# An FFN whose up projections use seven products for a 2x2 block, with each down visit in two halves

## What is computed

```python
h = _rms(x, norm_g[l, 2]) * (1.0 + scale_f) + shift_f
a, g = jnp.split(h @ ffn_w_in[l], 2, axis=-1)          # 2048 -> 2 x 5632
x = x + (gate_f * _rms((jax.nn.silu(a) * g) @ ffn_w_out[l], norm_g[l, 3])).astype(x.dtype)
```

## Time and profile before

| | |
|---|---|
| median of 3 runs | 2585.65 us (2585.51 to 2586.03) |
| span of the profiled execution, first to last instruction | 2583.7 us |
| PE, DVE, ACT, Pool busy | 99%, 78%, 53%, 10% of the span |
| instructions | 34752, of them 12080 matmuls |
| data moved | 611 MB, mean 237 GB/s |

### The profile page before, as it was taken

The page is one execution under the profiler, slowest core; times in us unless marked ns, Lnnn a source line. Parts: engine busy times, 40 slices in busy tenths (PEclk is TensorE's granted clock), DMA queues, the critical chain, the costliest instruction groups (busy, mean ns, idle before and its releaser), DMA issues.

```text
span 2583.7 us, 34752 instructions
## 1 busy us (share of the span) xinstructions
PE 2564.6 (99%) x12080; PEld 2129.4 (82%) x12080; DVE 2003.3 (78%) x2580; ACT 1369.5 (53%) x1809; POOL 252.5 (10%) x312
## 2 busy tenths in 40 slices
PE   9999999999999999999999999999999999999998
PEld 8888888888888887888888777888788888888887
DVE  6898788788878889876686888787856666666898
ACT  6545566656665656455556444444644444444444
POOL 0021022223222000080000000000000000000000
PEclk9999999999999999999999999999999999999999
DMA  9667788878787986756555775799566666666785
GB/s 319 227 216 253 228 278 265 282 256 309 255 288 252 318 275 211 265 172 224 174 178 168 254 242 195 247 313 319 175 205 194 192 192 194 193 191 192 259 299 191
DMA packets 278364, 611.08 MB, mean 237 GB/s; under 512 B 19916, under 2 KB 21136, under 8 KB 276336
## 3 DMA queue, kind: packets, MB, share of 16 engines
q1 hardware_dynamic: 273696, 583.53, 69.2%
q0 software_dynamic: 4416, 26.13, 2.8%
q10 hardware_dynamic: 144, 0.01, 0.0%
HBM read 599.08 MB, written 11.29 MB: 236 GB/s over the span
## 4 chain that ended last, share of the span: by engine, by line
PE 92%; DVE 4%; ACT 1%; DMA 1%; issue 1%; SPq 0%; DVEq 0%; ACTq 0%
PE ps L670 92%; DMA w_raw<-in_w_in 1%; DVE w_lo L2111 1%; DVE arena L2106 1%; ACT w_hi L1338 1%; PE ps L807 0%; DVE arena L3104 0%; DMA w_raw<-in_ffn_w_out 0%; PE ps L828 0%; DVE arena L2132 0%; DVE x L2132 0%; ACT arena L1379 0%; PE ps L1254 0%; DVE x L2106 0%; DVE mod_parts L2254 0%
## 5 line engine op out<-in xcount | busy, mean ns | idle before, releaser
L1338 ACT ACTIVATE w_hi<-w_raw 128x1024 fp32r<-128x1024 f32 (+1 forms) x898 | 948.3, 1057 | 1135.5 <-PE ps L670 1037.4
L2111 DVE TENSOR_TENSOR w_lo<-w_raw,w_hi 128x1024 fp32r<-128x1024 f32 x809 | 1001.3, 1240 | 473.0 <-ACT w_hi L1338 468.8
L670 PE MATMUL ps<-w_hi,hop_part 128*128 128x512 f32 x4264 | 1334.2, 391 | 3.2 <-DVE w_lo L2111 2.0
L670 PEld LDWEIGHTS ps<-w_hi,hop_part 128*128 128x128 f32 x4264 | 800.3, 188 | 176.4 <-issue 5.1
L670 PE MATMUL ps<-w_lo,hop_part 128*128 128x512 f32 x2132 | 829.6, 389 | 0.0
L670 PEld LDWEIGHTS ps<-w_lo,hop_part 128*128 128x128 f32 x2132 | 400.3, 188 | 81.5
L670 PE MATMUL ps<-w_hi,hid_hi_part 128*128 128x512 f32 x992 | 387.1, 390 | 0.0
L670 PE MATMUL ps<-w_lo,hid_hi_part 128*128 128x512 f32 x992 | 386.0, 389 | 0.0
L670 PE MATMUL ps<-w_hi,hid_lo_part 128*128 128x512 f32 x992 | 386.0, 389 | 0.0
L2106 DVE SCALAR_TENSOR_TENSOR arena<-arena,cs 128x768 f32<-128x768 f32 x240 | 245.9, 1025 | 0.3
L670 PE MATMUL ps<-hop_part,w_hi 128*128 128x512 f32 (+1 forms) x992 | 236.1, 380 | 2.0 <-ACT w_hi L1338 1.1
(11 more groups left out here) (335 smaller groups left out, 1352.5 us busy)
## 6 DMA issues: line engine op xcount, KB each, us to landing
arena<-in_ada_w SPq DMA_DIRECT2D x256, 384.0 KB, 5.2
w_raw<-in_ffn_w_in SPq DMA_DIRECT2D x176, 512.0 KB, 4.4
w_raw<-in_w_up SPq DMA_DIRECT2D x128, 512.0 KB, 4.3
w_raw<-in_w_down SPq DMA_DIRECT2D x128, 512.0 KB, 4.9
w_raw<-in_w_gate SPq DMA_DIRECT2D x128, 512.0 KB, 4.4
w_raw<-in_ffn_w_out SPq DMA_DIRECT2D x88, 512.0 KB, 4.5
w_raw<-in_w_out SPq DMA_DIRECT2D x64, 512.0 KB, 5.3
w_raw<-in_wide_columns SPq DMA_DIRECT2D x64, 512.0 KB, 4.1
```

What stands on the lines that cost most here:

```text
L670: return nc.tensor.matmul(o, w, r, start=start, stop=stop, skip_group_check=True)
L1338: return nc.scalar.activation(o, i, ACT.Copy, scale=scale)
L2111: V.tensor_tensor(w_lo[:, j % LEAD, :, 0:cols], w_raw[:, j % RAW, :, 0:cols], w_hi[:, j % LEAD, :, 0:cols].bitcast(F32), ALU.subtract).the ...
```

## The change

The up projections of eight of the eleven blocks are computed in another form. Activations (two halves of 128 tokens) and weights (two halves of a unit's rows; gate columns and up columns side by side) are seen as 2x2 blocks, and their product is made from seven block products instead of eight, with sums of blocks on both sides. One gate unit and the up unit of the same rows form a group (64 groups). Its seven pieces of weights are `11`, `12`, `s2`, `s4`, `s1`, `s3`, `22`; each gets three matmuls into a bank of its own, so that seven PSUM banks are held through a block and the eighth, `VISIT_BANK`, takes the down projection and the transposes.

Pool makes the sums: four sums of activation blocks once, three sums of weight blocks for each group (two in place in the raw weights), and four sums and products at the end of a block. DVE and ACT split the seven pieces (`form_hi`, `form_lo`: pieces in twos, the seventh alone) and put the seven banks together at a block's end (`end_step`, `end_first`, `end_fifth`, `end_silu`). PE now turns the product (`turn_product`), 4 transposes for each half of the tokens. A down visit is one column part for one half of the tokens, 12 matmuls, three groups behind; its halves of 6 come behind the fifth and the seventh product of a group, and DVE adds each visit's bank to `ACC_TOK` (`drain`). The second pair of raw weights, the sums and the split sums lie in parts of `arena`, and the split down weights in `x` and `row_store`; so x is parked in DRAM and brought back. The loops are written out instead of looped.

The core of the diff (`...` marks what is left out: the same waits for the stages behind, and names):

```diff
+SEVEN = ("11", "12", "s2", "s4", "s1", "s3", "22")
+SEVEN_BANK = (4, 5, 6, 0, 1, 2, 3)
+VISIT_BANK, SPARE_BANK = 7, 4
+SUPERS = FFN_SUPER - 3
+GROUPS = SUPERS * UA
+VISITS = GROUPS
+SHIFT = 3
+E_RING = 3
...
+def forms(g, n=0):
+
+    return R_FORM * 8 + 4 * g + n
...
+    PAIR_RAW = (w_raw[:, 0:2], flat(T(56, 8)).rearrange("p (n k c) -> p n k c", n=2, k=UK))
+
+    def t_sums(g):
+
+        return flat(T((64, 68)[g % 2], 4)).rearrange("p (k c) -> p k c", k=2)
+
+    def piece(w, first, n):
+
+        return w[:, :, :, :].rearrange("p l k c -> p (l k) c")[:, first:first + n]
+
+    def form_raw(g, i):
+
+        raw = PAIR_RAW[g % 2]
+        return (raw[:, 0], raw[:, 1], t_sums(g), raw[:, 0, 1:2])[i]
+
+    FORM_AT, FORM_N = (0, 2, 4, 6), (2, 2, 2, 1)
+    FORM_SUMS = (0, 2, 1, 3)
+
+    def left(name, i, hl):
+
+        if name[0] == "s":
+            return s_forms[:, int(name[1]) % 4, hl, i]
+        t, k = int(name[0]) - 1, int(name[1]) - 1
+        return hop[:, UK * i + k, hl, t * P:(t + 1) * P]
+
...
+        def load_pair(g):
+
+            c, i = 1 + g // UA, g % UA
+            for n, col in enumerate((c * COLS, FFN + c * COLS)):
+                sp.dma_start(PAIR_RAW[g % 2][:, n], w_ffn_in[i, :, :, col:col + COLS]).then_inc(pair_in[g % 2], 16)
+
+        def load_down(u):
+
+            d, n, k = u // UA, u % UA // UB, u % UB
+            sp.dma_start(w_raw[:, 2 + u % 2], w_ffn_out[UB * d + k, :, :, n * COLS:(n + 1) * COLS]).then_inc(down_in[u % 2], 16)
+
+        sp.wait_ge(sem["lo_ready"], R_FFN * 8 + 14)
+        load_pair(0)
+        sp.wait_ge(sem["hop_ready"], HOP[7] + KT + 4)
+        load_pair(1)
+        sp.wait_ge(sem["lo_ready"], forms(1))
+        load_pair(2)
+        for s in range(GROUPS):
+            if s < 2:
+                sp.wait_ge(sem["lo_ready"], R_FFN * 8 + 15 + s)
+            else:
+                sp.wait_ge(sem["down_lo"], HEADS + s - 1)
+            load_down(s)
+            if s + 3 < GROUPS:
+                sp.wait_ge(sem["lo_ready"], forms(s + 2))
+                load_pair(s + 3)
...
+        def bank_free(c, p):
+
+            if c == 0:
+                if p >= 3:
+                    pe.wait_ge(drained[0 if p < 5 else 1], H_FFN + 2)
+            else:
+                read = (("end_act", 4, 1), ("end_dve", 5, 1), ("end_dve", 5, 2), ("end_dve", 5, 4), ("end_act", 4, 3),
+                        ("end_dve", 5, 3), ("end_dve", 5, 5))[p]
+                pe.wait_ge(sem[read[0]], HEADS + read[1] * (c - 1) + read[2])
+
+        def turn_product(c, t):
+
+            if c == 0:
+                pe.wait_ge(drained[1], H_FFN + 2)
+            else:
+                pe.wait_ge(sem["end_pool"], 4 * (c - 1) + 3 + t)
+            if UA * c + 1 + t > SHIFT:
+                pe.wait_ge(sem["visit_drained"], HEADS + UA * c + 1 + t - SHIFT)
+            if t == 1:
+                pe.wait_ge(sem["hid_ready"], base + 2 * c + 1)
+            for f in range(FT):
+                m = nc.tensor.transpose(PS[VISIT_BANK][:, f * P:(f + 1) * P], PROD_TOK[:, t, f * P:(f + 1) * P], ident)
+            m.then_inc(sem["hid_turned"], 1)
+
+        def group(g, visited=None):
+
+            c, i = g // UA, g % UA
+            for p, name in enumerate(SEVEN):
+                if p % 2 == 0:
+                    pe.wait_ge(sem["lo_ready"], forms(g, p // 2 + 1))
+                if p == 2 and g == 0:
+                    pe.wait_ge(sem["hop_ready"], HOP[7] + KT + 4)
+                if i == 0:
+                    bank_free(c, p)
+                o = PS[SEVEN_BANK[p]][:]
+                wh, wl = (piece(w, p, 1)[:, 0] for w in (w_hi, w_lo))
+                mm(o, left(name, i, 0), wh, start=i == 0, stop=False)
+                mm(o, left(name, i, 0), wl, start=False, stop=False)
+                m = mm(o, left(name, i, 1), wh, start=False, stop=i == UA - 1)
+                if p % 2 or p == len(SEVEN) - 1:
+                    m.then_inc(sem["unit_done"], 1)
+                if p == 1 and i in (1, 2):
+                    turn_product(c, i - 1)
+                if p == 4 and visited is not None:
+                    visit(visited, g, 0)
+
+        def visit(v, s, b):
+
+            d, n, t = visit_of(v)
+            tail = v - (VISITS - SHIFT)
+            bank = SPARE_BANK if tail in (0, 2) else VISIT_BANK
+            if tail == 0 and b == 0:
+                pe.wait_ge(sem["end_act"], HEADS + 4 * (SUPERS - 1) + 1)
+            if v > 0 and b == 0:
+                pe.wait_ge(sem["visit_drained"], HEADS + (v - 1 if tail >= 0 else v))
+            if b == 0:
+                pe.wait_ge(sem["hid_ready"], base + turned_by(s))
+            o, rows = PS[bank][:], slice(t * P, (t + 1) * P)
+            u = UB * (v // 2) + b
+            pe.wait_ge(sem["down_lo"], HEADS + u + 1)
+            for r in range(UK):
+                k = UK * b + r
+                wh, wl = (down_weights(u, hl)[:, r] for hl in range(2))
+                mm(o, hid_hi[:, d % 2, k, rows], wh, start=k == 0, stop=False)
+                mm(o, hid_hi[:, d % 2, k, rows], wl, start=False, stop=False)
+                m = mm(o, hid_lo[:, d % 2, k, rows], wh, start=False, stop=k == FT - 1)
+            m.then_inc(sem["visit_used"], 1)
+
+        for s in range(GROUPS + SHIFT):
+            if s < GROUPS:
+                group(s, s - SHIFT if s >= SHIFT else None)
+            elif s >= SHIFT:
+                visit(s - SHIFT, s, 0)
+            if s >= SHIFT:
+                visit(s - SHIFT, s, 1)
+
...
+        def form_hi(g, i):
+
+            act.wait_ge(sem["unit_done"], forms(g - 1, i + 1))
+            if i == 0:
+                act.wait_ge(pair_in[g % 2], 16 + 32 * (g // 2 + 1))
+            else:
+                act.wait_ge(sem["sums_made"], HEADS + 4 + 3 * g + FORM_SUMS[i])
+            copy(piece(w_hi, FORM_AT[i], FORM_N[i]), form_raw(g, i)).then_inc(sem["hi_ready"], 1)
+
...
+        for s in range(-1, GROUPS + 2):
+            if 0 <= s - 2 < VISITS:
+                down_hi(s - 2)
+            if super_end(s) is not None:
+                end_first(super_end(s))
+            next_hi(s, 0)
+            if s % UA in (1, 2) and 0 < s < GROUPS:
+                up_hi(s // UA, s % UA - 1)
+            if super_end(s) is not None:
+                end_silu(super_end(s), 0)
+            if after_end(s) is not None:
+                end_silu(after_end(s), 1)
+            next_hi(s, 1)
+            if super_end(s) is not None:
+                end_fifth(super_end(s))
+            next_hi(s, 2)
+            next_hi(s, 3)
+        act.wait_ge(sem["end_pool"], 4 * SUPERS)
...
+        def form_lo(g, i):
+
+            dve.wait_ge(sem["hi_ready"], forms(g, i + 1))
+            V.tensor_tensor(piece(w_lo, FORM_AT[i], FORM_N[i]), form_raw(g, i), piece(w_hi, FORM_AT[i], FORM_N[i]).bitcast(F32),
+                            ALU.subtract).then_inc(sem["lo_ready"], 1)
...
+        def down_lo(u):
+
+            dve.wait_ge(sem["down_hi"], HEADS + u + 1)
+            V.tensor_tensor(down_weights(u, 1), w_raw[:, 2 + u % 2], down_weights(u, 0).bitcast(F32),
+                            ALU.subtract).then_inc(sem["down_lo"], 1)
...
+        def drain(v):
+
+            d, n, t = visit_of(v)
+            bank = SPARE_BANK if v - (VISITS - SHIFT) in (0, 2) else VISIT_BANK
+            dve.wait_ge(sem["visit_used"], HEADS + 2 * v + 2)
+            V.tensor_tensor(ACC_TOK[:, t, part(n)], PS[bank][:], ACC_TOK[:, t, part(n)], ALU.add).then_inc(sem["visit_drained"], 1)
+
+        def end_step(c, k):
+
+            o, p, i, used, sig, count = (
+                (0, 1, 2, 1, "end_act", HEADS + 4 * c + 1),
+                (2, 2, 2, 2, "end_dve", HEADS + 5 * c + 1),
+                (1, 5, 2, 3, "end_dve", HEADS + 5 * c + 2),
+                (2, 3, 2, 2, "end_pool", 4 * c + 1),
+                (1, 6, 1, 4, "end_pool", 4 * c + 2))[k]
+            dve.wait_ge(sem["unit_done"], forms(UA * c + UA - 1, used))
+            dve.wait_ge(sem[sig], count)
+            if k in (0, 2) and c:
+                dve.wait_ge(sem["end_pool"], 4 * (c - 1) + 3 + k // 2)
+            V.tensor_tensor(end_tile(o), PS[SEVEN_BANK[p]][:], end_tile(i), ALU.add).then_inc(sem["end_dve"], 1)
+
...
+        for s in range(-1, GROUPS + SHIFT + 1):
+            if s == SHIFT + 1:
+                dve.wait_ge(sem["cleared"], 2)
+            if s > SHIFT:
+                drain(s - SHIFT - 1)
+            if 0 <= s - 2 < VISITS:
+                down_lo(s - 2)
+            end = super_end(s)
+            if end is not None:
+                end_step(end, 0)
+            next_lo(s, 0)
+            if s % UA in (1, 2) and 0 < s < GROUPS:
+                up_lo(s // UA, s % UA - 1)
+            if end is not None:
+                end_step(end, 1)
+            next_lo(s, 1)
+            if end is not None:
+                end_step(end, 2)
+            next_lo(s, 2)
+            if s == -1:
+                dve.wait_ge(sem["unit_done"], R_FFN * 8 + 2 * UA)
+                product(H_FFN)
```

(74 more changed lines are left out.)

152 lines of the change are left out of this document (103 added, 49 removed).

## The result

The changed kernel takes 2751.84 us (median of four runs, 2750.68 to 2752.19) against 2585.58 us for the kernel before on the same chip: a ratio of 1.0641, 95% interval 1.0625 to 1.0656. It is slower by 166 us. The forecast was 2762, in a range of 2683 to 2848. The profiled execution has a span of 2750.3 us and a mean granted clock of 0.983.

A forecast was written before the change was run, and what follows sets the result against it. PE bounds the kernel before; the prediction took DVE, taking turns with Pool's sums, to bound the changed FFN. 2583.7 + 168 for eight blocks + 8 for edges + 2.0 gave 2762 us, range 2683 to 2848.

The forecast's parts named there:

- PE's own work, 60.7 us a block: FFN block on PE: 264 matmuls, 59.8 us, plus eight transposes at 0.87 us; 7.6 us per group.
- DVE's own work, 5.75 a group and 4.2 at the end, 50.2: DVE's w_lo pieces and drain per group, seven PSUM adds at block's end; 50.2 us a block, hidden behind PE's 60.7.
- Taking turns: Pool and DVE alternate, one instruction at a time, when both read two SBUF operands; DVE adds with a PSUM operand are exempt.
- A group, 9.95: Per group in DVE's queue: 5.75 own work plus 4.8 of Pool's sums, less 0.6 hidden on the drain.
- My rival of the partial lock: Pool's sums block DVE for half their time; DVE needs 72 us per block, total 2649 us; 7%.
- The block's end, 6.7: At each block's end: 4.2 us of DVE and 4.8 of Pool, with 2.3 us overlapped.
- the links of the end run beside these: At a block's end, third add, Pool's sum, fourth add and freeing of seven banks run beside the counted work; no size given.
- A block, 86.3: FFN block of eight groups at 9.95 plus 6.7 at its end; 21.0 us more than 65.3, 168 us for eight.
- The edges, 8: Activation sums, unaccompanied last visits and parked x outside the steady blocks: 0 to 21 us, of which 8 taken.
- PE stays the bound: Rival: Pool's sums fall in DVE's gaps, costing DVE less than 15 us per block; 2553 us; 8%.
- PE's clock: Rival: PE, less busy, drops to 1.2 GHz in most groups, costing 336 us, about 3100 us; 4%.
- What the profile would show: PE near 90% busy, DVE near 100%, w_lo mean 1.7 to 1.9 us, drain 0.68, Pool's sums over 1.1 us longer each.

The follow-up runs named there:

- experiment 1: The changed kernel with Pool's three weight sums per group left out, only their signals kept: 2598.0 us, ratio 1.0049 to the kernel before.
- experiment 2: The changed kernel with each of Pool's three weight sums replaced by three memsets, which read nothing from SBUF: 2630.14 us, ratio 1.0172 to the kernel before.
- experiment 10: The changed kernel with none of Pool's seven sums (three weight sums, four at a block's end), waits kept: 2580.69 us, ratio 0.9979 to the kernel before.
- experiment 3: The changed kernel with the three weight sums of each group made by DVE instead of Pool: 2699.77 us, ratio 1.0441 to the kernel before.
- experiment 5: The kernel before, plus three unneeded Pool additions of the three sums' sizes, 64 times: 2591.32 us, ratio 1.0021 to the kernel before.
- experiment 6: The kernel before, plus unneeded Pool memsets, three in place of each addition of the three sums' sizes, 64 times: 2585.86 us, ratio 1.0000.
- experiment 4: The changed kernel with one more unneeded Pool subtraction of 512 elements per group: 2799.65 us, ratio 1.0827 to the kernel before.
- experiment 9: The changed kernel with only the third of Pool's weight sums left out, its count and wait kept: 2716.47 us, ratio 1.0506 to the kernel before.
- Experiment 8: The changed kernel with Pool's four sums and products at a block's end left out, waits kept: 2725.4 us, ratio 1.0531 to the kernel before.
- 7: The changed kernel with the two sets of transposes behind the fourth product of their groups, not the second: 2756.31 us, ratio 1.0656 to the kernel before.
- 11: The changed kernel with DVE's drain moved ahead of one w_lo in the two steps of a block before a transpose: 2759.8 us, ratio 1.0671.
- 12: The kernel with the three weight sums on DVE, with the drain moved ahead of one w_lo in two steps a block: 2702.98 us, ratio 1.0458.

## Why the prediction was right, and where its terms were off

- **PE's own work, 60.7 us a block, with 7.6 a group.** Right where it can be seen: 7.5 to 7.57 us a group in experiments 1, 2 and 10. A block of PE alone took 63.0 (experiment 10), 2.3 more than the sum. Most of that is the transposes: before, eight stood together for 0.87 us; now they come in two sets of four, and in experiment 10 a group with a set takes 8.85 us where the others take 7.54. That is 2.6 us a block and not 0.87. A set as it stands in experiment 1:

```profile
2039.47 0.39 PE L786 MATMUL ps<-w_hi,hop_part 128*128 128x512 f32 x1
2040.12 0.63 PE L1449 MATMUL ps<-const,arena 128*128 128x128 f32 x4 [0.26 <-issue]
2040.51 0.47 PE L786 MATMUL ps<-w_hi,s_forms 128*128 128x512 f32 x1
2040.82 0.39 PE L786 MATMUL ps<-w_lo,s_forms 128*128 128x512 f32 x1
```

  From the first of these starts to the last are 1.35 us; less two matmuls of 0.23 the set takes 0.90, twice its share of the 0.87.
- **DVE's own work, 5.75 a group and 4.2 at the end, 50.2.** Right: 51.4 us busy in a block with no sums (experiment 10), and 8.20 a group with 2.45 more to do (experiment 3).
- **Taking turns.** Shown by what was changed and what was not: only Pool's reads lengthen w_lo (experiments 1, 2, 5, 6), in a kernel without the change too, and one sum more or less changes a group in which DVE has no gap by 0.94 and 1.09 us (experiments 4 and 9). Both were sums of 512 elements; that the price grows with the length is not shown by itself.
- **A group, 9.95; measured 9.52.** The term that was mis-sized is Pool's 4.8 us. Its own time is 2.40 (a row that stands in the earlier trace rows, not in the earlier trace rows) + 2 x 1.29 = 4.98, a little more, but 0.2 us of a sum lies outside the turn. Experiment 9 shows that for the third sum; taken for all three, 4.98 - 0.6 - 0.6 on the drain = 3.78, against 9.52 - 5.75 = 3.77. The 0.6 on the drain was right: in the changed kernel Pool's second sum takes 1.60 us where it falls on a drain and 2.15 where it doesn't. My rival of the partial lock had the right kind and a wrong size: 12% of a sum is outside, not half.
- **The block's end, 6.7; measured 83.8 - 8 x 9.52 = 7.6.** Near in size, but by another mechanism. I added DVE's 4.2 and Pool's 4.8 and took off an overlap that I chose. Experiment 8 has Pool's part at 3.3, where the sum had 2.5 on net. But in experiment 9 the five groups around the end gave 2.2 us where the turns alone would give 5.5, and in experiments 2 and 3 the end grew (68.4 us a block for 65.2, and 12.6 over eight steady groups). They behave as a chain. In the changed kernel's block PE waits 5.14 us for a drain, then ScalarE 2.99 us for PE before a high half (at 2173.41), then DVE 1.71 us for that high half (at 2174.50). That "the links of the end run beside these" was the step that failed, at little cost.
- **What ends that chain is open.** Moving the transposes (7) or the drain (11, 12) only moved the wait. Only taking sums of Pool's away shortened it (8 and 9). The clock may be one link: after PE's stand it is at 0.50, and eight distances of matmuls, from 2166.31 to 2169.88 us, take 3.57 us where they would take 1.8 at 1.00. The 1.8 us in between are as long as DVE's wait of 1.71 right behind, but that was not tried alone.
- **A block, 86.3; measured 83.8.** 2.5 x 8 = 20 us too much, over.
- **The edges, 8; measured 18.** 2751.8 - 2585.6 - 8 x (83.8 - 65.3) = 18. In experiment 10 the same sum gives 13, in experiment 3 11. The bound of 21 held, my choice in it was too low, and this paid back half of the block's surplus: 2762 came within 10 us partly by luck, two errors of opposite sign. Of the 18, one wait is in the trace: before the last visits PE stands for 9.5 us until a down w_lo (L3385) is made, which DVE's queue has behind the last block's end adds (6.4 us in experiment 10); I had 0 to 9 for the end. The rest is open.
- **The rivals.** "PE stays the bound" needed Pool to cost DVE less than 15 us a block: it cost 78.5 - 51.4 = 27. Even at zero the time is 2581, not 2553, because I had a block of 60.7 there and 4 for the edges. PE's clock never fell for long: 0.96 over a block, by some stretches at 0.50.
- **What the profile would show.** The w_lo mean (1771 ns), the drain (678 ns) and DVE's share (78.5 of 83.8 us, 94%) are near what I named. Pool's sums grew by less than the 1.1 us each that I named: 0.3 us for the one on the drain, 0.9 and 1.0 for the others. PE is busy for 94% of the span where I said near 90, since I thought of the FFN alone (66.6 of 83.8 us is 79% there). I said that PE's idle time inside a group ends with a w_lo; the waits name the drain of the visit's bank more often, because DVE's queue has it behind the last w_lo:

```profile
PE ps L786 <- DVE arena L3406: 7.0, 5, 1.7
...
PE ps L786 <- DVE arena L3420: 2.7, 1, 2.7
```

No version that computes the right result beats the kernel before. With the sums on DVE the eight steady groups alone are 8 x 8.20 = 65.6 us, against 65.3 for a whole block before; with the sums on Pool it is 76. The saving would need the sums from somewhere that costs neither engine.
